# Down and output projections of a two-layer encoder on TensorE: each product of 512 columns issued as two of 256

## The reference

```python
for layer in range(DEPTH):                                   # DEPTH = 2
    hn = rmsnorm(h, mix_norm_pre[layer])
    proj = einsum('bsd,de->bse', hn, w_in[layer])            # 1024 -> 2048: u, q, k, v
    y_pool = pool_mixer(u, pool_w[layer], pool_scale[layer])
    y_na = neighbourhood_attention(q, k, v, na_rpb[layer])
    mix = einsum('bse,ed->bsd', concatenate([y_pool, y_na]), w_out[layer])   # output projection
    h = h + rmsnorm(mix, mix_norm_post[layer])
    hn = rmsnorm(h, ffn_norm_pre[layer])
    if layer == 0:                                           # dense, 1024 -> 4096 -> 1024
        f = einsum('bsf,fd->bsd', silu(hn @ w_gate) * (hn @ w_up), w_down)
    else:                                                    # top 2 of 8 experts, 1024 -> 3584 -> 1024
        f = moe_swiglu(hn, router, w_gate, w_up, w_down)
    h = h + rmsnorm(f, ffn_norm_post[layer])
```

## Time and profile before

| | |
|---|---|
| median of three runs | 1312.96 us (1312.72 to 1313.02) |
| the profiled execution, its own time | 1314.43 us |
| its span, from the first to the last instruction | 1312.6 us |
| mean granted TensorE clock over the span | 0.995 of full speed |
| TensorE busy | 1284.9 us (98%) |
| weight loads busy | 792.8 us (60%) |
| VectorE, ScalarE, GpSimd busy | 403.0, 286.0, 108.0 us |
| DMA | 443.50 MB, mean 338 GB/s |

### The profile page before, as it was taken

How to read it: one execution, slowest core, us unless ns; L and a number is a source line. 1 busy time by engine, 2 the same in 40 slices (tenths; PEclk the granted TensorE clock), 3 DMA queues, 4 the chain that set the end, 5 groups by cost and what they waited for, 6 DMA issues and landing times.

```text
span 1312.6 us, 31061 instructions
## 1 busy us (share of the span) xinstructions
PE 1284.9 (98%) x14401; PEld 792.8 (60%) x14401; DVE 403.0 (31%) x563; ACT 286.0 (22%) x433; POOL 108.0 (8%) x240
## 2 busy tenths in 40 slices
PE   8999999999999999999999999999999999999996
PEld 7988999999989863354353364345353354346333
DVE  6776555555575850030210120030030031031011
ACT  4665344444465730000000000000000000000101
POOL 4134300000000307300000000000000000000000
PEclk9999999999999989999999999999999999999998
DMA  9547855555543399999999999999999999999994
GB/s 303 219 163 214 265 192 193 193 193 193 193 155 144 135 424 427 425 421 399 426 425 426 425 424 425 427 424 424 425 426 425 425 424 425 426 426 423 426 424 165
DMA packets 66868, 443.50 MB, mean 338 GB/s; under 512 B 4504, under 2 KB 10656, under 8 KB 42160
## 3 DMA queue, kind: packets, MB, share of 16 engines
q1 hardware_dynamic: 64592, 433.58, 81.2%
q0 software_dynamic: 2144, 7.90, 2.1%
HBM read 439.36 MB, written 2.10 MB: 336 GB/s over the span
## 4 chain that ended last, share of the span: by engine, by line
PE 89%; DMA 4%; DVE 3%; ACT 2%; SPq 1%; issue 1%; ACTq 0%; DVEq 0%
PE psum L1074 38%; PE psum L1083 18%; PE psum L724 9%; PE psum L726 9%; PE psum L725 9%; DMA unit<-in_moe_w_down 3%; PE psum L1018 2%; PE psum L1029 1%; PE psum L821 1%; PE psum L812 1%; DMA ring<-in_w_in 1%; ACT pt L1227 1%; PE psum L753 1%; DVE hs L1515 0%; ACT prob_b L1288 0%
## 5 line engine op out<-in xcount | busy, mean ns | idle before, releaser
L1074 PE MATMUL psum<-unit,xT 128*32 128x448 f32 x5376 | 507.0, 539 | 0.1
L1074 PEld LDWEIGHTS psum<-unit,xT 128*32 128x32 f32 x5376 | 174.3, 110 | 327.5 <-issue 325.3
L1083 PE MATMUL psum<-unit,hid 128*32 128x256 f32 x4704 | 259.3, 379 | 3.7 <-DMA unit<-in_moe_w_down 3.7
L1083 PEld LDWEIGHTS psum<-unit,hid 128*32 128x32 f32 x4704 | 151.4, 110 | 109.1 <-DMA unit<-in_moe_w_down 5.6
L1733 DVE TENSOR_TENSOR hidp<-hid,psum 128x448 f32<-128x448 f32 x42 | 38.4, 914 | 535.4 <-PE psum L1074 535.4
L1421 DVE TENSOR_TENSOR w_lo<-ring,w_hi 128x2048 fp32r<-128x2048 f32 x64 | 148.3, 2323 | 120.3 <-ACT w_hi L1186 120.0
L724 PE MATMUL psum<-hT_hi,w_hi 128*128 128x256 f32 x656 | 182.8, 279 | 0.8 <-DVE qT L1541 0.7
L726 PE MATMUL psum<-hT_hi,w_lo 128*128 128x256 f32 x656 | 181.7, 277 | 0.0
L725 PE MATMUL psum<-hT_lo,w_hi 128*128 128x256 f32 x656 | 181.7, 277 | 0.0
L1186 ACT ACTIVATE w_hi<-ring 128x2048 fp32r<-128x2048 f32 x71 | 135.3, 1911 | 64.6 <-PE psum L726 52.8
L724 PEld LDWEIGHTS psum<-hT_hi,w_hi 128*128 128x128 f32 x656 | 123.5, 188 | 2.5 <-issue 1.0
(11 more groups left out here) (251 smaller groups left out, 942.5 us busy)
## 6 DMA issues: line engine op xcount, KB each, us to landing
unit<-in_moe_w_gate SPq DMA_DIRECT2D x64, 1792.0 KB, 33.1
unit<-in_moe_w_up SPq DMA_DIRECT2D x64, 1792.0 KB, 28.0
unit<-in_moe_w_down SPq DMA_DIRECT2D x64, 1792.0 KB, 32.7
ring<-in_dense_w_gate SPq DMA_DIRECT2D x8, 2048.0 KB, 9.2
ring<-in_dense_w_up SPq DMA_DIRECT2D x8, 2048.0 KB, 9.1
ring<-in_dense_w_down SPq DMA_DIRECT2D x8, 2048.0 KB, 8.7
ring<-in_w_in SPq DMA_DIRECT2D x6, 2048.0 KB, 8.6
ring<-in_w_out SPq DMA_DIRECT2D x4, 2048.0 KB, 8.5
```

The lines of the kernel that those rows point to most:

```text
L1074: ins = mm(bank(half, s)[quad(j)], xT[:, s, dt, :], w[:, at:at + FJ], start=dt == 0, stop=dt == DT - 1)
L1083: ins = mm(down_out[s][quad(j)], e[:, half, s, t, :], w, start=half == t == 0 and s != 2, stop=half == 1 and t == FT - 1, skip_group_check ...
```

## The change

The three places that made a product of 512 columns with `product` call a new function, `wide`, in its stead. It makes the same product over the first 256 columns (three matmuls) and then over the other 256 (three more). The start flag, which makes a bank's sums begin anew, is given to the first of the six alone, the stop flag to the last of each three. Nothing else differs: waits and signals stand where they stood, and products that already had 256 columns still call `product`.

```diff
+            def wide(dst, still, moving, start, stop):
+
+                for i in range(2):
+                    cut = slice(i * C2, (i + 1) * C2)
+                    for k, (a, b) in enumerate(((0, 0), (0, 1), (1, 0))):
+                        ins = mm(dst[:, cut], still[a], moving[b][:, cut], start=start and i == k == 0,
+                                 stop=stop and k == 2, skip_group_check=True)
+                return ins
...
                     for j in range(2):
-                        ins = product((pa, pb)[t][:, j * C4:(j + 1) * C4], still,
-                                      [a[:, et, j * C4:(j + 1) * C4] for a in w],
+                        ins = wide((pa, pb)[t][:, j * C4:(j + 1) * C4], still,
+                                   [a[:, et, j * C4:(j + 1) * C4] for a in w],
...
-                        return product((pa, pb)[t][:, j * C4:(j + 1) * C4], [a[:, e, t * P:(t + 1) * P] for a in src], w,
+                        return wide((pa, pb)[t][:, j * C4:(j + 1) * C4], [a[:, e, t * P:(t + 1) * P] for a in src], w,
...
-                    return product((pa, pb)[t][:, n * C4:(n + 1) * C4], still, w, b == c == f == 0,
+                    return wide((pa, pb)[t][:, n * C4:(n + 1) * C4], still, w, b == c == f == 0,
```

## The result

The changed kernel takes 1317.22 us in the median of six runs (1315.89 to 1318.06), the kernel before 1312.49 us in six runs beside them (1311.14 to 1313.02). The ratio is 1.0036, with a 95% interval of 1.0026 to 1.0046: slower by about 4.7 us. The forecast was 1311.2 us, and no change the likeliest case.

What follows compares the result with a forecast made beforehand. TensorE was taken as the bound, its matmul stream running at one of two cadences. Savings in downs, opening and layer 0's projection summed to -2.7 us, giving 1310.3 or 1311.7 us; forecast 1311.2, range 1310.0 to 1322.5 us.

Steps and rivals of the forecast that it cites:

- all short: Dense part and layer 0's output projection at 113.3 ns per 256-column matmul: -2.7 us, chance 0.45.
- all long: Rival: dense part entered at 117.8 ns per 256-column matmul and staying there: +7.9 us, chance 0.37.
- A sign of being wrong: Dense part: stretches between downs growing to 22.6 us, or the cadence changing within a stretch with no step of size.
- mixed and fixed-cost cases: Rivals: dense downs long, gate and up short, +1 to +2.4 us; or fixed cost per matmul, +1.3 us; together 0.18.
- the price of `wide` in the projections: Output projections: each 256-column matmul priced at 113.3 ns; layer 0's projection was to save 0.2 us.
- The upper end of the prediction's interval, +0.6: Layer 1's output projection: possible change of -0.2 to +0.6 us, kept as ends though nothing was counted.
- layer 1's projection isn't covered: Claim judged: layer 1's output projection lies beside expert loading, its change goes into slack and counts as nothing.
- The chance of slower, 0.39: Whole kernel: chance of a measurably slower time, made of the +7.9 us rival and a little of the +1 to +2.4 us one.

Runs made afterwards that it cites:

- `d_only`: 256-column products in the dense part alone, both output projections as in the kernel before: 1315.76 us, ratio 1.0017.
- `neutral`: Change in the dense part alone, plus one 256-column matmul, tokens for both operands, between each down and the up behind it: 1316.02 us, ratio 1.0020.
- `double`: Change in the dense part alone, plus two 256-column matmuls per down-up border, first tokens moving, then weights moving: ratio 1.0033, profile 1323.7 us.
- `open_step`: Kernel before plus one 512-column matmul, weights moving, ahead of the second half of gate 0: 1312.47 us, ratio 1.000.
- `step_long`: Dense downs at 256 columns except their last product; added weights-moving matmuls, one of 512 in gate 0, one of 256 ahead of up 0: 1312.45 us, ratio 1.0008.
- `p_only`: 256-column products in both output projections alone, dense part as in the kernel before: 1313.08 us, ratio 1.000.
- `forced_long`: Dense downs at 256 columns, ending in twelve 512s at down 0, three at later downs; one 256-column matmul added ahead of gate 2: ratio 1.0021.

## Why the prediction was wrong

**Wrong: both likely cases rested on a cadence that is only kept or left at the entry.** The step is the sentence that the stream "holds the one that it has over hundreds of matmuls", together with "the change takes out every step from 512 to 256 in the dense part". From these I drew two outcomes, all short (-2.7 us) or all long (+7.9), and put 0.45 and 0.37 on them. The rows allowed that for stretches within a down or within gate and up. They could not show a border from moving weights to moving tokens with 256 columns on both sides, for in the trace of before each such border in the dense part had 512 on its one side. In `d_only`, `neutral` and the changed kernel it turns the cadence over each time, so that neither case came, but half of each. A sign of being wrong that the prediction named did appear: up 2 with gate 3 took 22.62 us, and the cadence changed with no step of size. With the counts of the trace: 384 + 3 x 288 = 1248 matmuls at 117.8 ns and 1056 at 113.3 are 266.7 us, measured 266.8. The sum of the long case was right for a stream that stays long: `double` shows 273.2 us, of which its fourteen added matmuls are 1.6, so 271.6, where the sum gives 263.7 + 7.7 = 271.4. The price that the prediction put on the mixed and fixed-cost cases, 1313 to 1316 us, isn't what its own sums give: mixed is 1314.0 to 1316.8. (Long from 1314.43 is 1322.3, not 1322.4.)

I had looked at the border itself, and had the wrong reading of it: "All seven steps from 512 to 256 columns ... end in the short cadence" was put down to the step of size alone. One matmul of 512 columns amid the opening (`open_step`, `step_long`) leaves a long stream long, while one of 256 turns it. Size matters, but not alone.

**Wrong: the price of `wide` in the projections.** I took 113.3 ns, "the cadence of the stream that it stands in", against the nearest rows by the order of operands, which said 117.8. In the changed kernel and in `p_only`, layer 0's projection ran at 117.8 ns throughout, and layer 1's but for 22 matmuls in one of them, at +0.57 and +0.49 us. The upper end of the prediction's interval, +0.6, was near the value. What it had not asked is where the short cadence of the 512s there came from. In the kernel before, layer 0's projection begins long behind the small matmuls (three distances of 512 make 0.697 us from 84.30 us on) and is short from the next three on (0.687). With 256 columns it began long too and stayed so, in eleven of the twelve stretches that both layers have in the changed kernel and in `p_only`. Why the 512s leave the cadence and the 256s don't is open.

**Wrong: layer 1's projection isn't covered.** I counted nothing for it, because the DMA engines are full from 455 us on the earlier trace rows and the end waits for a load. The +0.49 us is still there at the first expert matmul (491.32 and 494.68 us) and at the last load, which is issued at 1261.45 us for 1258.13 and lands after 36.72 us for 36.82:

```profile
1261.45 36.72 DMA unit<-in_moe_w_down
```

A full queue of loads didn't take up the delay: SP issues each load when TensorE has freed a slot, so a later TensorE makes the loads later too.

**Right:** that durations mislead and distances between starts are the cost; the two cadences and their distances, which long stretches of all fourteen profiles show within 0.2 ns behind their first few matmuls; that the 576 added weight loads cost nothing of their own; that two of 256 at the short cadence are less than one of 512 (10.90 us for 10.99 in down 1); that the entry is open, and that no other engine becomes the bound. The Trainium skill gives an isolated matmul at full clock a fixed 2.5 ns beside its columns ("TensorE: Matmul & The Clock Gate", "Back-to-back issue gap"). By that alone a down of 96 would have been slower than one of 48; down 1 was not. The chance of slower, 0.39, came from a case with the right sign, a size of 7.9 us where 4.7 were measured, and the wrong mechanism: what there is right about it is luck. The range held the time only because it was made wide for that case.

**Open:** why the stream has two cadences at all, and why the turn comes with the moving operand's switch from the weights' buffers to the tokens'. The experiments exclude the code's place, the change of bank by itself and a meeting of both reads in the weight buffers. They don't say whether it is the address, the pattern or the timing of the reads. That a short stream, too, stays short over two switches rests on timed runs alone. Open as well is why before's profiled execution lies 1.9 us above its median, and that of the changed kernel 0.5 us.

## What to carry to other kernels

Measure a matmul's price as the distance between starts, in stretches cut where the instruction mix changes, and look whether equal stretches give equal numbers. If they don't, the stream has more than one state, and a change must be priced by what it does to the transitions between them: here the edit should have saved about 0.7 us of the dense part as it was entered in the profile, by the prices of its matmuls, and the borders that it altered made it 3.1 us longer. Where a change makes a combination that the trace has nowhere (here 256 columns on both sides of a switch of operands), price it in an interval that holds both states, stretch by stretch, and not only all or nothing.

## What the runs showed of the hardware

- A stream of 128x128 weight loads and matmuls in `F32R` at a granted clock of 1.00 (2.4 GHz) has two stable cadences: 113.3 or 117.8 ns a matmul of 256 columns, 228.9 or 233.3 of 512. At 256 columns each was held over up to 384 matmuls without a break (`d_only` short, the changed kernel long).
- At 256 columns, one switch of the moving operand from weight buffers to token buffers turned it over, both ways, in each of 22 borders seen (seven each in the changed kernel, `d_only` and `neutral`, one in `step_long`), and once more in `forced_long`, where the added matmul made the short stream long. Two switches in a row left it (14 borders in two profiles, all in long streams). The border the other way, from moving tokens to a down, never turned it. With three, twelve or 48 matmuls of 512 at a down's end the up behind it was short in every profile; a single 512 amid gate 0 left a long stream long twice.
- The end of a program can hang on TensorE's sequencer: with its loop over skipped code it reached the end 14.8 us behind the start of the last matmul in one profile and 7.1 to 8.6 us in the other thirteen.
